# Reordering a mixer's attention stream on TensorE by the size of the stationary tile

## The reference

```python
def hybrid_mixer(h, w_in, w_gate, ...):
    ... = jnp.split(h @ w_in, offs, axis=-1)
    o_a = stick_breaking_attention(sb_q, sb_k, sb_v)           # 4 heads
    o_b = nsa_attention(...)   # 8 query heads in 2 groups: compressed, selected and window attention, gated
    o_c = dsa_attention(...)   # 4 heads, one key head; keys picked by an index score (top 128 of 512)
    g_a, g_b, g_c = jnp.split(jax.nn.sigmoid(h @ w_gate), 3, axis=-1)
    merged = g_a * (o_a @ w_br_a) + g_b * (o_b @ w_br_b) + g_c * (o_c @ w_br_c)
    return merged @ w_out

# stick-breaking: A[t,s] = sigmoid(z_ts) * prod_{s<j<t} (1 - sigmoid(z_tj)), s < t
log_1m = where(past, log_sigmoid(-z), 0)
tail = cumsum(log_1m, reverse=True) - log_1m
w = where(past, exp(log_sigmoid(z) + tail), 0)
```

## Time and profile before

| what | value |
|---|---|
| median of 3 runs | 3533.93 us (3533.31 to 3536.26) |
| profiled execution | 3532.96 us |
| its span, first to last instruction | 3531.4 us |
| granted clock of TensorE, mean | 0.994 |
| PE busy | 3468.6 us, 98% |
| DVE busy | 1950.6 us, 55% |
| ACT busy | 1470.7 us, 42% |
| chain that ended last | PE 89%, DVE 6%, ACT 3% |

### The profile page before, as it was taken

The page is one execution under the profiler, slowest core; times in us unless marked ns, Lnnn a source line. Parts: engine busy times, 40 slices in busy tenths (PEclk is TensorE's granted clock), DMA queues, the critical chain, the costliest instruction groups (busy, mean ns, idle before and its releaser), DMA issues.

```text
span 3531.4 us, 46478 instructions
## 1 busy us (share of the span) xinstructions
PE 3468.6 (98%) x16740; PEld 2753.1 (78%) x16740; DVE 1950.6 (55%) x3217; ACT 1470.7 (42%) x2210; POOL 174.2 (5%) x181
## 2 busy tenths in 40 slices
PE   9999999999999999999999999999999999999997
PEld 7888886667888888888866587888888777878886
DVE  5443466767544344434657775443368886545433
ACT  5432355654444234423456644443333434434421
POOL 0000000000100000000000001000000001020001
PEclk9999999999999999999999999999999999999999
DMA  4233522114422322234321043223422223323231
GB/s 143 95 101 102 163 99 72 43 52 161 140 95 96 107 96 96 100 105 146 110 85 51 28 168 136 99 99 103 142 96 90 84 72 111 114 66 101 96 106 65
DMA packets 99831, 356.06 MB, mean 101 GB/s; under 512 B 11823, under 2 KB 12079, under 8 KB 98920
## 3 DMA queue, kind: packets, MB, share of 16 engines
q1 hardware_dynamic: 83232, 300.16, 25.5%
q10 hardware_dynamic: 9416, 30.34, 2.6%
q0 software_dynamic: 7040, 23.66, 1.8%
HBM read 330.98 MB, written 26.80 MB: 101 GB/s over the span
## 4 chain that ended last, share of the span: by engine, by line
PE 89%; DVE 6%; ACT 3%; issue 2%; POOLq 0%; DMA 0%; POOL 0%; ACTq 0%; DVEq 0%; SPq 0%
PE bank L329 25%; PE bank L331 24%; PE bank L330 24%; PE bank L622 5%; PE bank L1106 1%; PE bank L1077 1%; DVE unit_lo L308 1%; PE bank L1086 1%; PE bank L1725 1%; PE bank L1181 1%; ACT unit_hi L303 1%; PE bank L1123 1%; DVE val L1906 1%; PE bank L1741 1%; PE bank L1168 1%
## 5 line engine op out<-in xcount | busy, mean ns | idle before, releaser
L308 DVE TENSOR_TENSOR unit_lo<-unit_raw,unit_hi 128x1024 fp32r<-128x1024 f32 x526 | 647.3, 1233 | 675.7 <-ACT unit_hi L303 665.2
L329 PE MATMUL bank<-h_hi,unit_hi 128*128 128x512 f32 x2416 | 954.3, 395 | 5.7 <-DVE h_lo L413 4.1
L331 PE MATMUL bank<-h_hi,unit_lo 128*128 128x512 f32 x2416 | 942.6, 390 | 0.0
L330 PE MATMUL bank<-h_lo,unit_hi 128*128 128x512 f32 x2416 | 942.4, 390 | 0.0
L303 ACT ACTIVATE unit_hi<-unit_raw 128x1024 fp32r<-128x1024 f32 x526 | 552.3, 1052 | 351.2 <-PE bank L331 338.4
L329 PEld LDWEIGHTS bank<-h_hi,unit_hi 128*128 128x128 f32 x2416 | 454.7, 188 | 117.6 <-issue 23.5
L331 PEld LDWEIGHTS bank<-h_hi,unit_lo 128*128 128x128 f32 x2416 | 454.6, 188 | 95.7
L330 PEld LDWEIGHTS bank<-h_lo,unit_hi 128*128 128x128 f32 x2416 | 454.9, 188 | 93.2 <-issue 1.7
L329 PE MATMUL bank<-act_hi,unit_hi 128*128 128x512 f32 x880 | 342.3, 389 | 0.0
L330 PE MATMUL bank<-act_lo,unit_hi 128*128 128x512 f32 x880 | 342.3, 389 | 0.0
L331 PE MATMUL bank<-act_hi,unit_lo 128*128 128x512 f32 x880 | 342.3, 389 | 0.0
(11 more groups left out here) (325 smaller groups left out, 4502.6 us busy)
## 6 DMA issues: line engine op xcount, KB each, us to landing
unit_raw<-in_units SPq DMA_DIRECT2D x564, 512.0 KB, 3.3
gates_kept<-gate_z POOLq DMA_DIRECT2D x32, 256.0 KB, 2.3
sig_ab<-gates_kept ACTq DMA_DIRECT2D x16, 512.0 KB, 3.6
bias_rows<-bias_once POOLq DMA_DIRECT2D x2, 3840.0 KB, 19.3
x_kept<-x ACTq DMA_DIRECT2D x3, 2048.0 KB, 11.2
x<-x_kept ACTq DMA_DIRECT2D x3, 2048.0 KB, 8.7
xc<-xc ACTq DMA_DIRECT2D x16, 256.0 KB, 4.3
bias_t<-bias_rows POOLq DMA_DIRECT2D x16, 256.0 KB, 3.8
```

The costliest lines, as they stand in the source:

```text
L308: nc.vector.tensor_tensor(w_lo[u % SLOTS][:], raw[u % SLOTS][:], w_hi[u % SLOTS][:].bitcast(F32), ALU.subtract).then_inc(unit_lo, 1)
L329: nc.tensor.matmul(out_ap, w_h, r_h, start=first, stop=False)
L330: nc.tensor.matmul(out_ap, w_h, r_l, start=False, stop=False)
L331: return nc.tensor.matmul(out_ap, w_l, r_h, start=False, stop=last)
```

## The change

Within a pair of slots PE's products are put in the order of their tile: 64x128 first (scores, then Z), then 128x128 (gate products, turns, sums and PV), then 128x64 (values, spread, compressed out), then index and compressed scores. For that:

- values are issued in odd slots only, two tiles together: those turned in slots q - 2 and q - 1;
- Z moves from slots 0, 2, 4 to 2, 4, 6 and stands right behind the scores; DVE reads it in the same slot (2, 4, 6 instead of 1, 3, 5), right behind its reduction;
- the spread moves one slot on, to two slots behind `weigh`; compressed out moves from slot 12 to 13; the merge of a group moves one slot on in b = 0;
- sums and PV move ahead of values and spread in their slot;
- the ring's order and ACT's list follow.

```diff
-    Z_MADE, Z_READ, SUM_MADE, SUM_READ = (0, 2, 4), (1, 3, 5), (11, 13, 15), (12, 14, 16)
+    Z_MADE, Z_READ, SUM_MADE, SUM_READ = (2, 4, 6), (2, 4, 6), (11, 13, 15), (12, 14, 16)
...
     def spread(q):
 
-        return weighted(q - 1)
+        return weighted(q - 2)
 
     def merged(q):
 
-        return next((g for g in GROUPS if q == 4 * last_batch(*g) + 5 + g[0] + LAG + 1), None)
+        return next((g for g in GROUPS if q == 4 * last_batch(*g) + 5 + max(g[0], 1) + LAG + 1), None)
...
-    CMP_SCORES, CMP_SHIFT, CMP_EXP, CMP_SCALE, CMP_TURN, CMP_OUT = 3, 5, 7, 9, 10, 12
+    CMP_SCORES, CMP_SHIFT, CMP_EXP, CMP_SCALE, CMP_TURN, CMP_OUT = 3, 5, 7, 9, 10, 13
...
         for q in range(SLOT_END + 1):
             b, at = divmod(q, JOBS)
             if q < SLOTS2 and q % 2 == 0:
                 scores((q, q + 1))
+            if b < TB:
+                stick_z(b, at)
             if gate_piece(q):
                 gate_products(pe, r, *gate_piece(q))
-            if tile_of(q - LAG) and not opens_group(q):
-                values(*tile_of(q - LAG))
             if tile_of(q):
                 turn(*tile_of(q))
-            if opens_group(q):
-                values(*tile_of(q - LAG))
+            if b < TB and at == CMP_TURN:
+                compressed_turn(b)
+            if b < TB:
+                stick_sums(b, at)
+            if q % 2 == 1:
+                for done in (q - LAG, q - LAG + 1):
+                    if tile_of(done):
+                        values(*tile_of(done))
+            if spread(q):
+                spread_weights(*spread(q))
+            if b < TB and at == CMP_OUT:
+                compressed_values(b)
             for bh in index_heads(q):
                 index(*bh)
             if b < TB and at == CMP_SCORES:
                 compressed(b)
-            if b < TB and at == CMP_TURN:
-                compressed_turn(b)
-            if b < TB and at == CMP_OUT:
-                compressed_values(b)
-            if spread(q):
-                spread_weights(*spread(q))
-            if b < TB:
-                stick(b, at)
```

More of the change, by code:

```diff
@@ L979, in ring_uses @@
         uses = [("turn", *tile_of(q))] if tile_of(q) else []
+        if b < TB and at == CMP_TURN:
+            uses += [("turned", b, 0)]
+        if spread(q):
+            uses += [("spread", *spread(q))]
+        if b < TB and at == CMP_OUT:
+            uses += [("compressed out", b, 0)]
         uses += [("index", *bh) for bh in index_heads(q)]
@@ L1154, in compressed_values, with stick_z @@
             mm.then_inc(s["ring_in"], 1)
-        def stick(h, slot):
+        def stick_z(h, slot):
             half = slice(64 * (h % 2), 64 * (h % 2) + 64)
@@ L1170, in stick, with stick_sums @@
                 mm.then_inc(s["sb_z"], 1)
+        def stick_sums(h, slot):
             if slot in SUM_MADE:
@@ L1280, in mix2_act @@
                 nc.scalar.activation(prob_t[t % 3][:], src[:], ACT.Copy).then_inc(s["ring_out"], 1)
+            if b < TB and at == CMP_TURN:
+                src = arrives(("turned", b, 0))
+                if b > 0:
+                    act.wait_ge(s["ring_in"], ring_no["compressed out", b - 1, 0] + 1)
+                nc.scalar.activation(cmp_t[:], src[:, 0:256], ACT.Copy).then_inc(s["ring_out"], 1)
+                stick_high(b)
+            if spread(q):
+                g, w = group_no(*spread(q)), 512 if spread(q)[1] < 2 else 256
+                src = arrives(("spread", *spread(q)))
+                if g >= 2:
+                    act.wait_ge(s["o_out"], g - 1)
+                nc.scalar.activation(spread_c[g % 2][:, 0:w], src[:, 0:w], ACT.Copy).then_inc(s["ring_out"], 1)
+            if b < TB and at == CMP_OUT:
+                src = arrives(("compressed out", b, 0))
+                nc.scalar.activation(block_of(2, 4, b), src[:].rearrange("p (i t) -> p i t", i=4), ACT.Copy).then_inc(s["ring_out"], 1)
             for ib, h in index_heads(q):
@@ L1292, in mix2_act @@
                     nc.scalar.activation(cmp_s[:, g * P:(g + 1) * P], src[:, 0:P], ACT.Copy).then_inc(s["ring_out"], 1)
[L1293 to L1307, removed]
             if b < TB and at == CMP_EXP:
@@ L1360, in stick @@
                 ins.then_inc(s["sb_zm"], 1)
+        def stick(h, slot):
             if slot == SP_SLOT:
```

11 lines of the change are left out of this document (2 added, 9 removed).

## The result

The changed kernel takes 3554.07 us, the median of 4 runs (3550.66 to 3556.22), against 3534.66 (3533.31 to 3536.26) for the kernel before, measured beside it: a ratio of 1.0058, 95% interval 1.0045 to 1.0070. It is 19 us slower. The forecast was 3537.5, with a range to 3550: the sign was the one I gave 28%, and the time is outside the range.

A forecast was written before the change was run, and what follows sets the result against it. PE bounds b = 0, 1 and the tail, with DVE nearly level from mid b = 2 to slot 75. Per layer -3.3 us plus 5.3 for clock falls is +2.0, +4 in all: 3533.9 + 4 = about 3537.5, range 3522 to 3550.

The forecast's parts named there:

- the one I gave 28%: Whole kernel: slower by more than about 0.2% (7 us), 28%.
- What the order saves on PE: Attention stream: 89 fewer changes of tile size per layer save 14.5 us per layer on PE, 29 for both.
- The wait for `sb_lo`: First sums in slot 11 of every b: waits of 5.0 us in all go to about 2.5, 2.5, 3.4 and 3.9.
- The walk by b at full clock: Each query block of the stream, savings less new waits: net -3.3 us per layer, -6.6 for both.
- two reads of the sums: b = 2, slots 13 and 15: sums reach `sb_d` before DVE has read the last ones, about 1.1 us each.
- The clock: Behind the new slot 11 waits: 3 to 4 half-clock falls per stream instead of one, 3.5 x 1.5 = 5.3 us.
- C: Rival: `sb_lo` waits make the clock fall in every slot 11 and slot 13 of b = 2, 3; 3541 to 3550; 25%.
- A: Rival: PE is the bound throughout and the tile-size switches come back in full; 3505, or some 3514; 10%.
- B: Rival: order works as walked, clock falls no oftener or where PE is idle anyway; 3522 to 3530; 19%.
- the choice of 50% for no change: Whole kernel: time within about 0.2% (7 us) of the kernel before, given 50%.

The follow-up runs named there:

- the filled kernel: Changed kernel with 9, 11, 12 and 14 added unread products ahead of the `sb_lo` wait in slot 11 of b = 0 to 3; 3541.09 us.
- the changed kernel with a table of its own: Changed kernel with only GATE_FILL changed, spreading the same gate products otherwise over the slots (59 pieces instead of 76); 3510.31 us, ratio 0.9937.
- the old one with a table of its own: Kernel before with only GATE_FILL changed, spreading its gate products otherwise over the slots (47 pieces instead of 76); 3500.41 us, ratio 0.9908.

## Why the prediction was wrong

**What the order saves on PE: right.** 14.5 us per layer forecast, 13.5 measured at full clock. Value tiles of 0.48 and 0.43, Z without an extra, changes at 0.09 to 0.10 leaving and 0.05 to 0.10 arriving hold. The Trainium skill ("TensorEngine Tiling (Array Packing)", Key Properties) ties a drain to a change of mode and not of tile. Z behind scores, both 64x128, shows 0.11 us from product to product, which agrees. Whether the price of going from one size to another is that drain, no run here shows.

**The wait for `sb_lo`: right.** About 2.5, 2.5, 3.4, 3.9 forecast, 2.56, 3.05, 3.33, 3.73 measured: 12.3 and 12.7 in all, with b = 1 half a microsecond short. And 3.3 us from sums to scores.

**The walk by b at full clock: wrong, and this is the step that failed.** It gave +0.3, -1.2, -0.3 and -2.1 (b = 3 with its tail), -3.3 us per layer, against a kernel before with its one fall in b = 3. With the falls of the changed kernel filled away the second stream shows, against the same kernel before, +1.5, +0.7, +1.2 and -1.0: 252.7 - 250.2 = +2.5. That is 5.8 us per layer off, 11.6 in all, some in every b. Of the 5.8, 1.0 is the smaller saving on PE, and 4.8 are waits: 17.4 us more of them came, and a walk of -3.3 leaves room for 12.6 (14.5 less the 1.9 that it wins over a kernel before without its fall, taken at 1.4). `sb_lo` is not where they came from. Its growth was forecast at 7.3 and came at 7.5.

By b, from the idle times of the filled kernel:
- b = 0: the wait for a row maximum in slot 2 is 1.3 us, where 0.5 stood for `unit_lo`, and the gate copy is waited for once more, 0.9 us in slot 12. The walk had 0.4 for slot 2 and nothing for the other.
- b = 1: 0.9 us for the weights of slot 19, where the walk had 0.2 for small waits and even let the gate copy's shrink by 0.4 (it stayed at 0.42); and the half microsecond at `sb_lo`.
- b = 2: the walk's own terms don't give its -0.3. They are -3.6 saved, +0.8 where DVE sets slots 48 to 50, +1.9 in slot 11 and +2.2 for two reads of the sums. That is +1.3, and +1.2 was measured. That is partly luck: only one of the two reads came (1.1), and the gate copy (0.9) and the compressed turn (0.75) stood in for the other.
- b = 3: 1.3 and 0.6 us for exponentials ahead of a transpose, 1.4 for a read of the sums, 0.3 each for scores and compressed scores and 0.4 more before the compressed turn, where the walk took DVE as the bound and its net as 0.

So the failed step is that what PE saves was taken as won wherever PE was busy, with the hand-overs to ACT and DVE put at nothing but for a few. In slot 12 of b = 0, for one, compressed out, 1.0 us long (563.31 to 564.33), stood between two gate products; now they follow each other, and the later one waits 0.86. The hint was in the rows: PE 98% busy with DVE waiting 36.8 us looked like a PE bound with slack on the others. But the chains from PE through ACT and DVE back to PE take their time, and PE's work between their ends was what covered them; in the changed kernel with a table of its own the gate copy's 3.6 us go to 1.7 and the compressed turn's 1.8 to nothing, by other work put in front of them.

**The clock: right in kind, short in number.** 3.5 falls of 1.5 us per stream, 10.6 us in all, were forecast; ten pieces came, six and four. At the 1.4 us of the filled kernel they cost 14.4, 3.8 more than forecast. Together with the 11.6 this is 15.4 of the miss of 16.6 us (3554.1 - 3537.5). Of the other 1.2, 0.4 is the forecast's own sum, which gives 3537.9, and 0.8 is within the spread of the executions. Not foreseen were falls with no wait over 0.4 us close ahead, behind small products in slots 3 and 4 of b = 0 and b = 3; and that the wait of 2.56 us in b = 0 had none (with Z taken back it had one in both streams). The prediction said that the new waits "are all like the last or longer". The Trainium skill ("TensorE: Matmul & The Clock Gate", Part 4: PE-mode transpose) says that a transpose doesn't count for the clock in the way that other work does. The fall inside a row of index scores, transposes and values in slots 16 to 19 of b = 2 is compatible with it. The one behind 64-row scores and Z in b = 0 is not of that kind: from 531.99 to 539.87 us no transpose stands in the timeline.

**The rivals.** C had the place and the mechanism, and nearly the price per fall (1.5 to 1.7 us, against 1.2 to 1.4); it took the walk's -3.3 for granted as well, and so ended at 3550. A is out in the changed kernel, where waits take back what is saved. B is out: the clock fell five times as often.

**And the choice of 50% for no change** rested on the walk's small terms adding up to nearly nothing. They were all bounded from one side, by what a saving brings at most.

## What to carry to other kernels

When an order of work on the busy engine gets denser, look at every hand-over to another engine and back, and add up the work that stands between the two ends in the new order: each chain whose cover shrinks below its length is a new wait, though the engine is 98% busy. A product that has to wait goes last among those that don't, even if that costs changes of tile size: here four more a layer, by the prices above under 1 us a layer, against 24 us won in all. And after a change of order, refit the filler work before judging: here another filler table was worth 33 us, and no new order that was tried beat the old one with a table of its own.

## What the hardware showed that was not expected

- PE's granted clock fell to 1.2 GHz with no wait close ahead: behind 2.7 us of 64-row products (32-column compressed scores, scores, Z), 7.9 us after the last wait ended, and behind index scores, transposes and values, 13 us after it. In one kernel that second place ran 10.2 us at half clock. And behind the wait of 2.56 us in b = 0 there was no fall in either stream, where with Z taken back there was one in both.
- The same place in the two streams of one execution need not do the same: at 539.87 us the clock fell, in the second stream, with the same instructions and waits, it did not. So a comparison by the trace has to set half-clock stretches apart before it compares stretches.
- 46 useless products per layer made the kernel 13 us faster than the same waits left idle.
